# Expert weights loaded and awaited in halves of chunks from the fifth pair on, and one room for both gate rows

## The reference, cut to what matters

```
for l in range(2):
    mod = silu(c) @ ada_w[l] + ada_b[l];  sh1, sc1, gt1, sh2, sc2, gt2 = split(mod, 6)
    x = x + gt1 * token_mixer(modulate(rms_norm(x, g1[l]), sh1, sc1))
    t = modulate(rms_norm(x, g2[l]), sh2, sc2)
    # top group of 4, then top 2 of its 8 experts; per expert e and its tokens:
    #     (silu(t @ w1[e]) * (t @ w3[e])) @ w2[e] * weight
    x = x + gt2 * hier_moe(t)
return rms_norm(x, final_g)
```

## Time and profile before

| what | value |
|---|---|
| three runs, us | 2288.28, 2283.88, 2286.8 (median 2286.8) |
| profiled execution, us | 2283.03, of which the span is 2281.2 |
| PE busy | 2249.4 us (99%) |
| DVE, ACT, POOL busy | 1057.5, 461.1, 74.4 us |
| moved by DMA | 672.52 MB, mean 295 GB/s over the span |
| DMA bytes of the SP queue | 649.45 MB |

### The profile page before, as it was taken

The page is one execution under the profiler, slowest core; times in us unless marked ns, Lnnn a source line. Parts: engine busy times, 40 slices in busy tenths (PEclk is TensorE's granted clock), DMA queues, the critical chain, the costliest instruction groups (busy, mean ns, idle before and its releaser), DMA issues.

```text
span 2281.2 us, 26770 instructions
## 1 busy us (share of the span) xinstructions
PE 2249.4 (99%) x11302; PEld 1377.5 (60%) x11302; DVE 1057.5 (46%) x2098; ACT 461.1 (20%) x1041; POOL 74.4 (3%) x131
## 2 busy tenths in 40 slices
PE   9999999999999999999999999999999999999998
PEld 6569547886497459997533433335999743333343
DVE  4578756668588567675311111125767421111122
ACT  3411003358111011230211111101122021111111
POOL 2000000010000000000000000000000000000000
PEclk9999999999999999999999999999999999999999
DMA  7378725354689515246999999995424899999997
GB/s 296 116 313 358 309 76 202 149 184 162 246 346 407 181 54 211 98 185 256 410 427 428 428 427 427 427 419 210 175 78 168 344 426 427 427 427 428 427 427 285
DMA packets 59318, 672.52 MB, mean 295 GB/s; under 512 B 7521, under 2 KB 7809, under 8 KB 18865
## 3 DMA queue, kind: packets, MB, share of 16 engines
q1 hardware_dynamic: 51888, 649.45, 69.2%
q0 software_dynamic: 7296, 21.21, 2.7%
HBM read 667.37 MB, written 3.26 MB: 294 GB/s over the span
## 4 chain that ended last, share of the span: by engine, by line
PE 89%; DMA 7%; DVE 3%; issue 0%; POOL 0%; ACT 0%; SPq 0%; DVEq 0%; POOLq 0%; ACTq 0%
PE ps L101 86%; DMA ring<-in_exp_w 5%; DVE arena L114 1%; DVE arena L117 1%; PE ps L350 1%; DMA arena<-ssm_rows 1%; PE ps L3112 1%; DMA ring<-in_ada_w 0%; PE ps L639 0%; DMA ring<-in_attn_w_in 0%; PE ps L2139 0%; DVE X L117 0%; DVE arena L110 0%; PE ps L1328 0%; POOL small L117 0%
## 5 line engine op out<-in xcount | busy, mean ns | idle before, releaser
L101 PE MATMUL ps<-arena 128*64 128x512 f32 (+5 forms) x4612 | 1075.9, 446 | 12.6 <-DVE arena L117 4.6
L101 PEld LDWEIGHTS ps<-arena 128*128 128x128 f32 (+2 forms) x4612 | 536.5, 168 | 425.3 <-issue 393.5
L101 PE MATMUL ps<-ring,arena 128*64 128x512 f32 (+2 forms) x1592 | 501.8, 583 | 1.5 <-DMA ring<-in_exp_w 1.5
L101 PE MATMUL ps<-XTGB,ring 128*128 128x256 f32 (+1 forms) x2032 | 382.5, 344 | 0.0
L101 PEld LDWEIGHTS ps<-XTGB,ring 128*128 128x128 f32 x2032 | 333.5, 191 | 43.8 <-issue 9.5
L101 PEld LDWEIGHTS ps<-ring,arena 128*64 128x64 f32 (+1 forms) x1592 | 185.0, 151 | 240.7 <-issue 236.4
L122 DVE COPY arena<-ps 128x512 f32<-128x512 f32 (+5 forms) x133 | 63.3, 496 | 401.1 <-PE ps L101 282.3
L121 ACT COPY arena<-ps 128x512 f32<-128x512 f32 (+3 forms) x187 | 85.0, 473 | 690.2 <-PE ps L101 283.6
L117 DVE TENSOR_TENSOR arena<-ps,arena 128x256 f32<-128x256 f32 (+5 forms) x290 | 127.1, 475 | 119.1 <-PE ps L101 89.0
L101 PE MATMUL ps<-XTGB,arena 128*128 128x128 f32 (+2 forms) x736 | 178.4, 396 | 0.0
L101 PE MATMUL ps<-ring,XTGB 128*128 128x512 f32 (+3 forms) x484 | 166.4, 498 | 1.9 <-DMA ring<-in_attn_w_in 1.8
(11 more groups left out here) (162 smaller groups left out, 1050.6 us busy)
## 6 DMA issues: line engine op xcount, KB each, us to landing
arena<-in_exp_w SPq DMA_DIRECT2D x96, 2048.0 KB, 28.9
ring<-in_exp_w SPq DMA_DIRECT2D x64, 2048.0 KB, 28.0
ring<-in_mlp_w SPq DMA_DIRECT2D x25, 2048.0 KB, 11.4
ring<-in_ada_w SPq DMA_DIRECT2D x20, 2048.0 KB, 9.5
XTGB<-in_exp_w SPq DMA_DIRECT2D x16, 2048.0 KB, 28.5
ring<-in_ssm_w_in SPq DMA_DIRECT2D x12, 2048.0 KB, 8.2
ring<-in_w_in SPq DMA_DIRECT2D x12, 2048.0 KB, 8.0
ring<-in_gate_w SPq DMA_DIRECT2D x12, 2048.0 KB, 7.9
```

Of the source, the lines that this page charges most:

```text
L101: return self.e.matmul(o, lhsT=lhsT, rhs=rhs, start=start, stop=stop, skip_group_check=True)
```

## The change

Three edits.

1. **Halves.** From pair 4 on (`HALVES = 4`), every pair of slabs is loaded by `chunk_halves`: the first half of the chunks of expert 0, the same of expert 1, then the two second halves, 1 MB each, with a semaphore of its own for the second half (`ringh`). The `exp_w3` and `exp_w2` of pair 15 keep their old halves. PE awaits the second halves in the middle of a block (at c == 4, at f == 2). A slot is taken and its last tenant awaited as before; the second halves are issued when both slots of the pair have been.
2. **One room.** `GATE[2]` and `GATE[5]` are one room, outside the slots. The experts' row is loaded by POOL at the head of the expert stage (`moe_pool`), once the mixer's row has been used; the mixer's row of layer 1 once the experts' row of layer 0 has been used.
3. **A slot sooner.** Slot NRING + 5 is free with the two "extra" rooms, and stands behind them and ahead of NRING + 4 and NRING + 3 in turn. The final gain is still loaded into its last 1024 floats, under the name `FINAL`, after the slot's last tenant.

```diff
--- before.py
+++ after.py
@@ -221,6 +221,7 @@
                      "fox_fb", "mla_g", "abias", "router_b", "rw", "dmask", "srow", "se0", "se1", "se2", "out"):
             sems[name] = ctx.enter_context(nc.semaphore("s_" + name))
         for i in range(NRING + 7):
+            sems[f"ringh{i}"] = ctx.enter_context(nc.semaphore(f"s_ringh{i}"))
             sems[f"ring{i}"] = ctx.enter_context(nc.semaphore(f"s_ring{i}"))
         for e in ("pe", "act", "dve", "pool"):
             for st in STAGES:
@@ -269,6 +270,21 @@
                         hs = slice(h * n // 2, (h + 1) * n // 2)
                         src, o = src[:, :, hs], o[:, :, hs]
                     sp.landed(sp.e.dma_start(o, src), f"half{sem + j}" if h else f"ring{place[key]}",
+                              ("w half" if h else "w", key))
+
+        def chunk_halves(sp, keys, name, offs, kc, n):
+
+            for h in range(2):
+                for key, off in zip(keys, offs):
+                    if h == 0:
+                        i, was = ring.take(key)
+                        if was is not None:
+                            sp.wait_ge(at("free", was))
+                        shape[key] = (kc, n)
+                    i = ring.home[key]
+                    f = slice(h * SLAB // 2, (h + 1) * SLAB // 2)
+                    src = d[name][off:off + P * SLAB].rearrange("(p f) -> p f", p=P)
+                    sp.landed(sp.e.dma_start(ring.bufs[i][:, f], src[:, f]), f"ringh{i}" if h else f"ring{i}",
                               ("w half" if h else "w", key))
 
         def load_behind_halves(sp, keys, name, offs, kc, n):
@@ -1636,7 +1652,9 @@
                 C[name] = arena.get(consts[name])
         ctab, stab = C["rope2c"], C["rope2s"]
         posf = small[:, 40:42]
-        GATE = {2: arena.ap[:, ASZ - D:ASZ], 5: arena.get(D)}
+        gate_row = arena.get(D)
+        GATE = {2: gate_row, 5: gate_row}
+        FINAL = arena.ap[:, ASZ - D:ASZ]
         gb = arena.get(24)
         xbase = arena.pos
         hrows = arena.get(2, D)
@@ -1706,8 +1724,7 @@
             pool.wait_ge(at("XT", 3, 1))
             pool.landed(pool.e.dma_start(C["cm"], d["const_cm"]), "late", "late")
             pool.landed(pool.e.dma_start(C["dmask"], d["const_dmask"]), "dmask", ("dmask", 0))
-            for i in (2, 5):
-                gate_rows(pool, 0, i)
+            gate_rows(pool, 0, 2)
             pool.landed(pool.e.dma_start(gb, d["gate_b"][0:P, :]), "gate_b", ("gate_b", 0))
             ada_b_pool(pool, 1, ab1)
             keep_mod(pool, 1)
@@ -2125,6 +2142,8 @@
                 ring.bufs[NRING + j] = arena.ap[:, xbase + j * SLAB:xbase + (j + 1) * SLAB]
                 ring.tenant[NRING + j] = ("extra", l)
                 ring.turn.append(NRING + j)
+            ring.tenant[NRING + 5] = ("extra", l)
+            ring.turn.append(NRING + 5)
             for n in range(2):
                 slab(sp, ("ow", l, n), "out_w", (l * 2 + n) * P * SLAB, 8, 512)
 
@@ -2751,8 +2770,7 @@
         def mix_pool(pool, l, nn):
             pool.stage(f"mix{l}")
             if l:
-                gate_rows(pool, 1, 2, at("free", last_over_gate[0]))
-                gate_rows(pool, 1, 5, at("xy ready", 0, NP - 1, 1))
+                gate_rows(pool, 1, 2, at("xy ready", 0, NP - 1, 1))
                 pool.wait_ge(at("free", last_over_mask[0]))
                 pool.landed(pool.e.dma_start(C["dmask"], d["const_dmask"]), "dmask", ("dmask", 1))
             pool.wait_ge(at("rqk", l, 1))
@@ -2856,6 +2874,7 @@
 
 
         LAST = (3, 7, 11, 13)
+        HALVES = 4
         HALVED = [[(nm, l, 0, j) for nm in ("exp_w1", "exp_w3") for j in range(2)] for l in range(2)]
         last_over_gate, last_over_mask = {}, {}
 
@@ -2990,9 +3009,8 @@
             return [at("sum", l, NG + 1, t, n) for n in range(2)]
 
         def moe_sp(sp, l):
-            for j, until in ((5, "gate row"), (2, "router")):
-                ring.tenant[NRING + j] = (until, l)
-                ring.turn.append(NRING + j)
+            ring.tenant[NRING + 2] = ("router", l)
+            ring.turn.append(NRING + 2)
             ring.turn.append(NRING + 6)
             for i in range(NP):
                 if i == 2:
@@ -3003,6 +3021,8 @@
                     kc, n = ((8, 512), (8, 512), (4, 1024))[k]
                     if all(ring.tenant[s] in HALVED[l] for s in ring.turn[0:2]):
                         load_behind_halves(sp, keys, nm, offs, kc, n)
+                    elif i >= HALVES and (k == 0 or i < NP - 1):
+                        chunk_halves(sp, keys, nm, offs, kc, n)
                     elif k and i == NP - 1:
                         slabs_in_halves(sp, keys, nm, offs, kc, n, k == 1, 2 * (k == 1))
                     else:
@@ -3020,13 +3040,14 @@
 
         def moe_pool(pool, l, nn):
             pool.stage(f"moe{l}")
+            gate_rows(pool, l, 5, at("free", ("gate row", l)))
             pool.wait_ge(at("rows", nn - 1, 0), at("rows", nn - 1, 1))
             pool.landed(pool.e.dma_start(dkeep[l], X), "keep", ("keep", l))
             if l == 0:
                 pool.landed(pool.e.dma_start(gb, d["gate_b"][P:2 * P, :]), "gate_b", ("gate_b", 1))
             else:
                 pool.wait_ge(at("free", last_over_gate[l]))
-                pool.landed(pool.e.dma_start(GATE[2], bcast(d["final_g"][0:1, :])), "gb", ("gb", "final"))
+                pool.landed(pool.e.dma_start(FINAL, bcast(d["final_g"][0:1, :])), "gb", ("gb", "final"))
             general(pool, l, flag_reg(pool, l), general_pool)
             rms_pool(pool, nn)
 
@@ -3096,7 +3117,7 @@
                 pe.wait_ge(at("w", (nm, l, i, 0)), at("w", (nm, l, i, 1)))
                 for c in range(8):
                     pe.wait_ge(at("xg ready", l, i, c // 4 * 4 if i else c // 2 * 2))
-                    if c == 4 and i == NP - 1 and nm == "exp_w3":
+                    if c == 4 and i >= HALVES:
                         pe.wait_ge(at("w half", (nm, l, i, 0)), at("w half", (nm, l, i, 1)))
                     for j in range(2):
                         ins = pe.mm(ps[64 * j:64 * j + 64, :], xg[:, c, 64 * j:64 * j + 64], w[j][:, c, :], c == 0,
@@ -3124,6 +3145,8 @@
 
                 if i < NP - 1:
                     for f in range(4):
+                        if f == 2 and i >= HALVES:
+                            pe.wait_ge(at("w half", ("exp_w2", l, i, 0)), at("w half", ("exp_w2", l, i, 1)))
                         for n in range(2):
                             ins = part(f, n)
                     pe.then_inc(ins, ("xy", l, i, 0), ("xy", l, i, 1), ("free", ("exp_w2", l, i, 0)),
@@ -3490,7 +3513,7 @@
                 v.wait_ge(at("rstd", 9, t), at("gb", "final"))
                 for n in range(2):
                     hs = slice(n * 512, (n + 1) * 512)
-                    v.then_inc(v.stt(X[:, t, hs], X[:, t, hs], rs2[:, t:t + 1], GATE[2][:, hs], ALU.mult, ALU.mult),
+                    v.then_inc(v.stt(X[:, t, hs], X[:, t, hs], rs2[:, t:t + 1], FINAL[:, hs], ALU.mult, ALU.mult),
                                ("out", t, n))
 
         def end_sp(sp):
```

## The result

The changed kernel takes 2296.32 us (median of 6 runs, 2293.26 to 2297.57), the kernel before 2285.82 beside it (2281.96 to 2288.28): ratio 1.0046, 95% interval 1.0034 to 1.0058. It is 10.5 us slower; +7.9 was forecast, 2294.7 as a time.

The account below looks back on a forecast made before the run. The prediction took the full weight stream to set the ends of the expert stages, with PE busy 99%. Layer 0 +4.5 and layer 1 +3.4 made +7.9 us on a median of 2286.8: 2294.7, range 2284.0 to 2300.0.

Parts of the forecast that it names:

- The stream sets the end: Expert stages: delay of the weight stream beyond its lead of 0.5 and 0.4 us delays the stage's end.
- The price of a half: Weight stream: a slab in two halves costs 0.074 us more; 68 slabs make 5.0 us per layer.
- Rival A: Full weight stream: halves cost nothing, so -2.1 us in all, 2284.7; chance 0.22.
- the 85 us a layer: Weight stream: estimated lengthening of a layer by the Trainium skill's 341 GB/s at 1 MB; set aside for the rows.
- PE's waits: Expert stages: old waits of 2.80 and 3.76 us go; one to two us appear in the last pair's exp_w3.
- Slot and gate row: Stage heads: a sooner slot gains 0 to 1.9 us, the gate row's load takes 1.2; taken as 0.
- The gap of the earlier trace: Stage heads: five us of stream at 261 and 265 GB/s instead of 427, 1.9 us lost; forecast to go.
- The gain: Final gain's load: frees 1.2 us of layer 1's stream; its cost at the end, 0, 0.6 or 5.7 us, taken as 0.
- the row of 3.8 us: Profile row of a load of the gain's size in a quiet queue, taken as nearest for the late gain.
- Layer 1: Layer 1's expert stage: +5.0 for halves, -0.4 for the stream's lead, -1.2 for the gain moved out: +3.4 us.
- Rival B: Expert stages: all old waits go and none returns at the last pair; -6.6 us, 2280.2; chance 0.05.
- C: Kernel's end: the gain's load is late as beside a full stream, 5.7 us on top, 2300.4; chance 0.08.

Follow-up runs that it names:

- Kernel 3: The changed kernel with both halves awaited ahead of a block's first matmul, except the last pair's exp_w3 and exp_w2; 2294.52 us, ratio 1.0052 to the kernel before.
- kernel 4: The changed kernel with halves from pair 15 on only, 2 newly halved slabs a layer instead of 68; 2283.20 us, ratio 0.9997 to the kernel before.
- kernel 5: Kernel 3 with each transfer taking 256 rows of 4 KB instead of 128 rows of 8 KB; 2315.69 us, ratio 1.0136 to the kernel before.
- kernel 1: The changed kernel without the new halves; slot sooner, one room and late gain stay; 2283.77 us, ratio 1.0000 to the kernel before.

## Why the prediction was right

**The stream sets the end: shown.** The last half of `exp_w3` lands 1532.51 - 1108.75 = 423.8 us into the stage, where it was 1523.98 - 1105.08 = 418.9: 4.9 us later, for 5.0 forecast. PE waits for it at the forecast place, 1.39 us for "one to two". In layer 1 it waits 1.34 us at the same matmul. Kernel 3 takes the early start away and loses nothing that can be told; kernel 4 takes the transfers away and gets the 5 us back.

**The price of a half: right, its making left open.** 0.074 us from eight halves at the head of a stage held in mid-stage: 421 GB/s, forecast 421 to 422. Rival A (halves for nothing) would have left 427. What the price consists of the forecast didn't say; kernel 5 puts it on the rows. The rule of the Trainium skill that the prediction sets against splitting ("DMA: Bandwidth & Descriptors", section "Bandwidth": at least 1 MiB) is met by halves of 1 MiB; the 85 us a layer that it estimates from the rate there were not seen: the stages are 4.5 and 3.8 us longer.

**PE's waits: half right.** The forecast was that those of the earlier trace rows go. They stayed, split over half blocks, and in layer 0 grew from 2.80 to 3.22 us: the stream is later along the whole stage, so PE meets it in the pairs 12 to 14 with halves too. This reading was wrong, but no term of the sum hung on it, since only the last wait counts.

**Slot and gate row: 0 forecast, 0 found.** The gap of the earlier trace rows is filled and the stages of kernel 1 have the length of before (436.9, and 436.6 with the gain's 1.2 gone).

**The gain: the mis-sized term.** I took 0, by the row of 3.8 us in a quiet queue; it took 5.4 us in a queue as quiet (8 GB/s a few us earlier, in the window above), like the gate row of 5.3, and cost 1.1. By 5.3 the prediction reckoned 0.6; most of the rest is what its working left out, 0.3 us from PE's last matmul to POOL's issue and 0.1 from the landing to DVE's start. The bounds 0 to 5.7 held it. With it the sum would have been 9.0, and the time 2295.8.

**Layer 1: +3.8 for +3.4,** within the scatter of a stage. Rival B (all waits gone) fell with PE's waits, C in its size: the gain is late, by 1.1 and not 5.7.

**Where it was luck.** The time came out 1.6 us above the forecast, the difference 2.6 (10.5 for 7.9): the kernel before measured 2285.82 beside the changed one and not the 2286.8 that the forecast stood on. The table of stages, not the nearness of the time, is what bears the forecast out.

## What to carry to other kernels

Where a stream of loads is full to the end, first find the load that the last consumer needs last: a wait that is removed ahead of it is only moved to it, and whatever makes the loads dearer is paid in full beyond that load's lead (0.5 and 0.4 us here). To start a consumer on half a tile paid nothing in the pairs before the last; what the halves that the last pair already had are worth, no run here tests. A small load that is put behind the last consumer to free the stream has to be compared with the slowest quiet transfer of its size, not the fastest.

## What the runs showed of the hardware

In these streams a row of a transfer costs some 9 ns beside its bytes even at 8 and 4 KB: whole slabs in rows of 16 KB stream at 427 to 428 GB/s, rows of 8 KB at 421, of 4 KB at 410. Slabs in two transfers of 64 partitions each, queued behind one another, move 214 GB/s, half of that. The Trainium skill says of two such transfers ("SBUF — State Buffer", section "Can I just issue two DMAs to hit both halves?") that one at partition 0 and one at partition 64 serialize; the rate of the run agrees, whether the two take turns it does not show.
